# When tile 0's dot products and the second table's rows are fetched in a one-core decoder step

## The chip, the cores and the metric

One core of a Trainium2 chip runs the whole program. The metric is the device time in microseconds of one execution. Three executions of the kernel before gave a median of 2046.18 us (2037.33 to 2052.13). A fourth, profiled one took 2047.33 us; its span from first to last instruction is 2045.5 us, and all rows below are of that one.

Five engines work side by side: TensorE (PE: matrix products, with PEld for its weight loads), VectorE (DVE), ScalarE (ACT), GpSimd (POOL) and SyncE (SP). POOL and SP only start transfers here. Each engine runs its own instructions in order; semaphores order them among each other.

## What is computed

The reference is one layer of a decoder on 512 prompt tokens and 32 sample tokens (8 sequences of 4 tokens). Cut to what matters:

```python
h = rmsnorm(x, attn_norm)
u, vn, q, k, v = mix_projection(h, w_in, ln_g, ln_b, pos)       # one projection feeds both mixers
a_out = gmlp_chunk(u, vn, w_s, b_s)
b_out = combine_branches(dilated window attention of q, k, v)   # sample tokens also read the cache
x = x + concatenate([a_out, b_out]) @ w_out
x = x + peer_ffn(rmsnorm(x, ffn_norm), w_q, sub_keys, u_tab, v_tab)
y = rmsnorm(x, final_norm)

def peer_ffn(x, ...):                      # for each token, 8 heads
    s = scores of x @ w_q against 2 x 128 keys
    top 16 of the 16 x 16 sums of the two top-16 lists -> eid, 16 of 16384 experts
    g = softmax(top scores)
    hid = gelu(dot(u_tab[eid], x))         # 128 rows of 1024 numbers for each token
    return sum over experts of g * hid * v_tab[eid]
```

All is float32. Each token reads 128 rows (4 KB each) of the first table u_tab and 128 of the second table v_tab; for 544 tokens that is 570 MB of the 670 MB that the kernel moves.

## The kernel before

The tokens are five tiles: tiles 0 to 3 are 128 prompt tokens each, tile 4 the 32 samples. The program is written out by hand, engine by engine.

Order of the work. Tile 0 is projected, attends, and has its output projection, queries and key scores first, ahead of all else (to about 146 us of the span). From then on the first table's rows of tile 0 can be fetched while the rest of the mixer runs: the projection of tiles 1 to 4 (to 299 us), then `attend(NG0, NG)`, the attention of tiles 1 to 3 and the samples (302 to 492 us). After attention come the output projections of tiles 1 to 4 (`project_out(t, c)` for two column halves c), their queries and key scores (13 more jobs, `queries(i)` and `key_scores(i)`, with 13 loads of `w_q`, the first 3 of which are started before attention ends), and the rest of the experts' work.

Experts. A fetch of the first table (`gather_u`) brings one row for each of 128 tokens, 0.52 MB, into a ring of UR = 6 buffers; DVE forms the 128 dot products with one instruction (L1431 in `dots_to`) and frees the buffer (`u_free`). There are 128 such fetches per prompt tile and 32 for the samples. A fetch of the second table (`gather_v`) brings the 128 rows of one token into a ring of VR = 6; PE multiplies it with that token's weights (`weigh`, L774) and frees it (`v_free`). The weights of tile t exist only once all dots of tile t are done: then come ACT's `gelu(t)`, DVE's `weights(t)`, PE's `turn_weights(t)`, ACT's `copy_weights(t)` and PE's `start_sum(t)`. `weigh_first(n)` makes the next n of tile 0's 128 weighings, and `made[0]` counts them. The 16 first-table fetches of a head wait until DVE has routed that head: `route(k)`, k = 8 t + h, is a chain of some 20 small instructions and needs the key scores of tile t, head h.

POOL's list. All fetches are started by POOL in one fixed order: the 128 first-table fetches of tile 0, then V_LEAD second-table fetches of tile 0, then first-table fetches of tile 1 alternating with the remaining second-table fetches of tile 0, and so on, tile t + 1 of the first table with tile t of the second. A fetch waits for a free buffer of its ring, and all behind it wait too.

Dots within attention. Attention runs over 26 groups: 18 pairs of heads, and after each second pair one sample sequence (8 of them). DVE makes for each group `mask_max`, `between(i, 0)`, `normalise`, `between(i, 1)`; `experts_between` puts dots there, as many as `dots_in_group(i, j)` says, from number 68 on, and at groups 1, 4 and 10 (`ROUTE_ATT`) one `route`. The samples read their cache: `load_vc(b)` fills a single buffer and starts only when the outputs of the sequence before are done.

Other tables. `NORM_AT` gives the dot before which DVE makes `norm_x2(t)` (the norm of tile t ahead of its queries). `ROUTE_STEP` gives, for group g of 16 dots, which heads are routed in it (head 10 after dot 136, 11 at 152, 12 at 168, 13 at 184, and so on). `EID_FIRST` is the number of tile 0's weighings that are made before PE turns tile 1's expert numbers (`turn_eid(1)`).

## Time and profile before

| | |
|---|---|
| median of three runs | 2046.18 us (2037.33 to 2052.13) |
| the profiled execution | 2047.33 us, span 2045.5 us |
| PE busy | 1513.8 us (74%), granted clock 0.913 of full |
| DVE busy | 1087.3 us (53%) |
| POOL busy | 1044.0 us (51%), 1088 of its 1119 instructions are table fetches |
| ACT busy | 215.8 us (11%) |
| DMA | 670 MB, 328 GB/s over the span; q0 (POOL's) 571.78 MB, q1 (SP's) 97.16 MB |

How to read it: a timeline row has the start, the length (us), the engine, the line, the operation, what is written and read, the count, and in brackets how long the engine had been idle and what released it. A POOL row is the time it takes to start a fetch, not to bring it. "L774 x4" is one weighing (two column halves, each in two passes). A row of the windows view gives, for a stretch of the span, each engine's busy time, then the granted TensorE clock, the busy share of the DMA engines, and GB/s.

### The profile page before, as it was taken

How to read it: one execution, taken by the hardware profiler on the slowest of the kernel's cores; microseconds unless marked ns; L12 is line 12 of the kernel's file. 1: busy time of each engine (PE TensorE's matmuls, PEld its weight loads, DVE VectorE, ACT ScalarE, POOL GpSimd, SP SyncE). 2: the span in 40 equal slices, each digit the busy share in tenths (PEclk: the TensorE clock that was granted, in tenths of full speed). 3: DMA queues.
4: the chain of work that ended last, by engine and by line, in shares of the span. 5: the costliest groups of instructions: out<-in, count | busy, mean ns of one | idle time of the engine just before them, and what ended most of it. 6: DMA issues, size and time to landing. Idle time of an engine off the chain costs nothing.

```text
span 2045.5 us, 16501 instructions
## 1 busy us (share of the span) xinstructions
PE 1513.8 (74%) x5398; PEld 547.7 (27%) x5398; DVE 1087.3 (53%) x2879; ACT 215.8 (11%) x610; POOL 1044.0 (51%) x1119
## 2 busy tenths in 40 slices
PE   7889977678977777775666676665666666777997
PEld 4475644444432223431111111111111111111221
DVE  2257868783356545526655556666666666422000
ACT  2411123343100000010100000010000000100000
POOL 3032332341555546346566666665555556666664
PEclk9799997778999889898899999998999888899999
DMA  9587868998998779769799999997888889999997
GB/s 320 198 315 253 310 248 328 343 405 329 332 385 329 279 282 377 297 230 377 288 369 372 357 368 357 360 382 284 325 317 321 323 319 339 342 367 363 370 363 280
DMA packets 213254, 670.00 MB, mean 328 GB/s; under 512 B 19600, under 2 KB 54656, under 8 KB 213040
## 3 DMA queue, kind: packets, MB, share of 16 engines
q0 software_dynamic: 157728, 571.78, 74.0%
q1 hardware_dynamic: 55440, 97.16, 13.3%
q8 instruction: 43, 0.70, 0.1%
q14 instruction: 43, 0.35, 0.0%
HBM read 663.26 MB, written 5.60 MB: 327 GB/s over the span
## 4 chain that ended last, share of the span: by engine, by line
PE 28%; DVE 19%; issue 16%; DMA 15%; POOL 14%; another core or an unknown queue 5%; ACT 2%; DVEq 0%; SPq 0%; ACTq 0%; POOLq 0%
POOL area_r L1576 14%; PE bank L774 10%; PE bank L549 6%; DMA area_r<-in_v_tab,eidT 6%; DMA area_r<-in_u_tab,eid 6%; DVE area_r L1431 6%; PE bank L719 3%; PE bank L672 2%; DMA area_w<-in_v_cache 2%; DVE area_w L1360 1%; DVE area_w L1358 1%; DVE rt L1361 1%; PE bank L492 1%; DVE rtu L1331 1%
## 5 line engine op out<-in xcount | busy, mean ns | idle before, releaser
L774 PE MATMUL bank<-area_r,area_c 128*32 128x512 f32 (+1 forms) x1632 | 697.5, 630 | 253.8 <-DMA area_r<-in_v_tab,eidT 223.1
L1431 DVE CUSTOM_DVE_ANT_0 area_r<-area_r,bank 128x1024 f32<-128x1024 f32 x544 | 648.0, 1217 | 423.3 <-DMA area_r<-in_u_tab,eid 364.4
L1576 POOL DMA_INDIRECT area_r<-in_u_tab,eid x544 | 515.1, 947 | 616.1 <-DVE hid L1431 381.1
L1576 POOL DMA_INDIRECT area_r<-in_v_tab,eidT x544 | 513.4, 944 | 369.9 <-PE bank L774 153.4
L774 PE MATMUL bank<-area_r,area_v 128*32 128x512 f32 (+1 forms) x544 | 285.1, 650 | 119.1 <-DMA area_r<-in_v_tab,eidT 107.2
L774 PEld LDWEIGHTS bank<-area_r,area_c 128*32 128x32 f32 (+1 forms) x1632 | 136.8, 111 | 788.3 <-DMA area_r<-in_v_tab,eidT 464.0
L549 PE MATMUL bank<-area_w,area_t 128*128 128x384 f32 (+1 forms) x448 | 160.8, 515 | 12.7 <-issue 8.5
L719 PE MATMUL bank<-area_t,area_w 128*128 128x128 f32 (+2 forms) x672 | 134.0, 360 | 22.6 <-ACT area_x L878 19.3
L774 PEld LDWEIGHTS bank<-area_r,area_v 128*32 128x32 f32 (+1 forms) x544 | 51.1, 114 | 312.5 <-DMA area_r<-in_v_tab,eidT 197.1
L719 PEld LDWEIGHTS bank<-area_t,area_w 128*128 128x128 f32 x672 | 101.9, 203 | 54.2 <-issue 42.6
L549 PEld LDWEIGHTS bank<-area_w,area_t 128*128 128x128 f32 x448 | 85.3, 194 | 78.8 <-issue 29.7
L878 ACT ACTIVATE area_x<-bank 128x384 f32<-128x384 f32 (+8 forms) x136 | 52.5, 409 | 397.1 <-PE bank L774 141.7
L1449 DVE RECIPROCAL small<-small 128x1 f32<-128x1 f32 x5 | 0.8, 160 | 143.8 <-ACT small L1106 143.8
L1073 ACT ACTIVATE tops<-tops 128x128 f32<-128x128 f32 (+1 forms) x5 | 1.5, 307 | 612.1 <-DVE rt L1361 354.3
L672 PE MATMUL bank<-area_w,area_t 128*128 128x512 f32 x128 | 59.3, 619 | 1.4 <-ACT area_t L878 0.7
L573 PE MATMUL bank<-area_r 64*128 64x128 f32 (+3 forms) x96 | 30.7, 716 | 25.3 <-DVE att L1273 23.3
L1431 DVE DVE_READ_ACCUMULATOR2_ANT hid<- 128x1 f32 x544 | 44.3, 81 | 0.0
L1264 DVE CUSTOM_DVE_ANT_0 area_x<-bank,area_c 128x256 f32<-128x256 f32 (+4 forms) x52 | 25.9, 535 | 30.4 <-PE bank L573 25.7
L878 ACT ACTIVATE area_t<-bank 64x128 f32<-64x128 f32 (+5 forms) x121 | 32.1, 276 | 73.0 <-PE bank L492 34.0
L1078 ACT ACTIVATE hid<-hid 128x128 f32<-128x128 f32 (+1 forms) x5 | 1.5, 293 | 353.7 <-DVE hid L1431 180.1
L878 ACT ACTIVATE area_w<-bank 128x256 f32<-128x256 f32 (+2 forms) x36 | 14.3, 399 | 213.3 <-PE bank L737 93.3
L1349 DVE MAX8 rt<-area_w 128x8 f32<-128x256 f32 (+1 forms) x40 | 17.0, 426 | 35.5 <-remote 25.9
(168 smaller groups left out, 1006.2 us busy)
## 6 DMA issues: line engine op xcount, KB each, us to landing
area_w<-in_w_q SPq DMA_DIRECT2D x21, 1024.0 KB, 8.0
area_w<-in_w_in SPq DMA_DIRECT2D x12, 1536.0 KB, 10.5
area_w<-in_k_cache SPq DMA_DIRECT2D x8, 1920.0 KB, 19.2
area_w<-in_v_cache SPq DMA_DIRECT2D x8, 1920.0 KB
area_r<-in_u_tab,eid POOLq DMA_INDIRECT x544
area_r<-in_v_tab,eidT POOLq DMA_INDIRECT x544
area_w<-in_w_out SPq DMA_DIRECT2D x4, 2048.0 KB, 9.6
area_w<-in_w_in SPq DMA_DIRECT2D x2, 2048.0 KB, 14.3
```

Source lines behind the costliest of these rows:

```text
L492: return pe.transpose(out, src, ident[0:n, 0:n])
L549: mm = pe.matmul(out_half(u)[0:n, 0:w], featT[:, k, a:a + n], w_now[:, k, 0:w], start=(k == 0), stop=(k == KD - 1))
L573: mm = pe.matmul(score_psum(u, n), qT[r0:r0 + HD, pr, t * P:(t + 1) * P], kT[r0:r0 + HD, pr, 0:n], start=True, stop=True)
L672: mm = pe.matmul(ps[0:n, :], featT[:, k, a:a + n], w(k, c * 512, (c + 1) * 512), start=(k == 0), stop=(t == 0 and k == KD - 1))
L719: mm = pe.matmul(half(4 + c)[:, 0:n], w[:, k, c * P:(c + 1) * P], featT[:, k, a:a + n], start=(k == 0), stop=(k == KD - 1))
L774: mm = pe.matmul(acc[CG * g:CG * g + m, e, :], wd[g][:, c * CG:c * CG + m], v_ring[s][:, e * 512:(e + 1) * 512], start=False, stop=False, ...
L878: return nc.scalar.activation(out, src, ACT.Copy, scale=scale)
L1264: return vec.tensor_tensor_reduce(out=out, in0=scores, in1=counts, scale=-1.0, scalar=3e38, op0=ALU.add, op1=ALU.min, accum_out=least)
L1331: vec.max_index(idx[c][0:n, 0:8], val[c][0:n, 0:8], sc[c])
L1358: link(vec.tensor_tensor(hot[0:n], digits[0:n].unsqueeze(3).to_broadcast(four), iota[0:n, :].rearrange("p (a b k) -> p a b k", a=1, b=1).t ...
L1431: vec.tensor_tensor_reduce(out=u_ring[s], in0=u_ring[s], in1=x_cur, scale=1.0, scalar=0.0, op0=ALU.mult, op1=ALU.add, accum_out=hid[t % 2] ...
L1576: nc.gpsimd.indirect_dma_start(out=ring[s], out_offset=None, in_=table, in_offset=bass.IndirectOffsetOnAxis(ap=where, axis=0)).then_inc(la ...
```

## The change

Attention holds 16 of tile 0's dots (2 before each sample group) in place of 59, so the dots reach number 84 there, not 127; the route groups too have their 2. The other 44 dots follow behind attention in `block.vector`, with the routes of heads 8 and 9 put after dots 112 and 120, and the norm of tile 1 before dot 100. Tile 0's weights come only then, so PE's `turn_weights(0)` and `start_sum(0)` move behind `project_out(2, 0)`, the 36 weighings that stood ahead of `project_out(2, 0)` and the four right behind it are gone from there, and ACT's `gelu(0)` and `copy_weights(0)` move likewise. In the jobs 8 to 12 `key_scores(i - 1)` now comes behind `queries(i)`, on PE and ACT. `v_free` is given its 6 buffers right after attention. V_LEAD goes from 30 to 6. The norms of tiles 2, 3, 4 come before dots 136, 142, 148 (they were at 152, 158, 165), and EID_FIRST from 104 to 100.

```diff
--- before.py
+++ after.py
@@ -64,11 +64,11 @@
 ROUTE_STEP = ({g: [g + 2] for g in range(8, 14)} | {15: [16], 16: [17, 18]} | {g: [g + 2] for g in range(17, 24)}
               | {g: [2 * g - 22, 2 * g - 21] for g in range(24, 31)})
 TOPS_ATT = 16
-NORM_AT = {SLOTS + 24: 2, SLOTS + 30: 3, SLOTS + 37: 4}
-V_LEAD = 30
+NORM_AT = {100: 1, SLOTS + 8: 2, SLOTS + 14: 3, SLOTS + 20: 4}
+V_LEAD = 6
 EARLY = 5
 EID_AT = 92
-EID_FIRST = 104
+EID_FIRST = 100
 
 
 def build(nc, x_p, x_s, k_cache, v_cache, gains, w_in, ln_gb, w_sT, b_sT, w_out, w_q, keysT, u_tab, v_tab,
@@ -328,11 +328,8 @@
         def dots_in_group(i, j):
             if not NG0 <= i < NG:
                 return 0
-            sample = ATT[GROUP[i][0]][0] == "s"
             before = i + 1 < NG and ATT[GROUP[i + 1][0]][0] == "s"
-            if j == 0:
-                return 2 if sample else 1
-            return 5 if before and i - NG0 not in ROUTE_ATT else 0
+            return 2 if j == 1 and before else 0
 
 
         JOBS = ([(h, [0]) for h in range(HEADS)] + [(h, [1]) for h in range(EARLY)]
@@ -831,25 +828,26 @@
             turn_eid(0)
             pe.wait_ge(w_out_again[0], 16)
             project_out(1, 0)
-            turn_weights(0)
+            pe.wait_ge(w_out_again[1], 16)
+            project_out(1, 1)
             pe.wait_ge(eidT_ready, 1)
-            start_sum(0)
-            pe.wait_ge(w_out_again[1], 16)
-            project_out(1, 1, 8)
-            weigh_first(8)
             turn_xn(1)
             pe.wait_ge(xnT_ready, 4)
             pe.wait_ge(x2_ready, 4)
             for i in range(HEADS, EARLY_END):
                 queries(i)
-                weigh_first(4)
-                key_scores(i)
+                if i > HEADS:
+                    key_scores(i - 1)
+            key_scores(EARLY_END - 1)
             for c in range(2):
                 pe.wait_ge(q_copied[c], EARLY_END)
             pe.wait_ge(s_ready, scores_through(EARLY_END - 1))
             for t in range(2, NT + 1):
                 if t < NT:
-                    project_out(t, 0, 4)
+                    project_out(t, 0, 4 if t > 2 else 0)
+                    if t == 2:
+                        turn_weights(0)
+                        start_sum(0)
                     project_out(t, 1, 4)
                 if t >= 3:
                     turn_xn(t - 1)
@@ -1151,20 +1149,23 @@
             clear(2)
             clear(3)
             attend(NG0, NG)
-            gelu(0)
             act.wait_ge(pv_done, len(ATT))
             act.wait_ge(v_out, 16 * (NT + 1))
             act.wait_ge(masked, len(ATT))
             clear(0)
             clear(1)
-            copy_weights(0)
             read_out(1)
             square_x2(1)
             copy_xnT(1)
             for i in range(HEADS, EARLY_END):
                 copy_q(i)
-                copy_s(i)
+                if i > HEADS:
+                    copy_s(i - 1)
+            copy_s(EARLY_END - 1)
             for t in range(2, NT + 1):
+                if t == 2:
+                    gelu(0)
+                    copy_weights(0)
                 if t < NT:
                     read_out(t)
                     square_x2(t)
@@ -1514,16 +1515,17 @@
                 dots_to(min(made_dots[0] + dots_in_group(i, j), SLOTS))
 
             attend(NG0, NG, experts_between)
-            dots_to(SLOTS)
             dve.wait_ge(pv_done, len(ATT))
             dve.sem_inc(v_free, VR)
             copy_eidT(0)
+            dots_to(112)
+            route(HEADS)
+            dots_to(120)
+            route(HEADS + 1)
+            dots_to(SLOTS)
             weights(0)
-            norm_x2(1)
             dve.wait_ge(xn_ready, 2)
             set_x(1)
-            route(HEADS)
-            route(HEADS + 1)
             for t in range(1, NT):
                 for h in range(STEPS[t]):
                     g = FIRST[t] + h
```

Three places show the order of instructions before and after. The first is PE's order from the end of attention: L492 (L489 of the change) is a turn (eidx: expert numbers, hid: weights, area_v: the normed tile), L672 (L669) with L681 (L678) an output projection's half, L759 (L756) `start_sum`, L774 (L771) weighings, L719 (L716) `queries`. Before:

```order
L492 MATMUL bank<-ident,eidx 128x128
L672 MATMUL bank<-area_w,area_t 128x512 x8
L681 MATMUL bank<-area_x,ident 128x512
L492 MATMUL bank<-ident,hid 128x128
L759 MATMUL bank<-area_w,ident 128x512 x2
L672 MATMUL bank<-area_w,area_t 128x512 x8
L681 MATMUL bank<-area_x,ident 128x512
L774 MATMUL bank<-area_r,area_c 32x512 x6
L774 MATMUL bank<-area_r,area_v 32x512 x2
L774 MATMUL bank<-area_r,area_c 32x512 x6
```

In the change, with rows left out where `queries`, `key_scores` and `project_out` follow each other:

```order
L489 MATMUL bank<-ident,eidx 128x128
L669 MATMUL bank<-area_w,area_t 128x512 x8
L678 MATMUL bank<-area_x,ident 128x512
L489 MATMUL bank<-ident,area_v 128x128 x8
L716 MATMUL bank<-area_t,area_w 128x128 x32
...
L489 MATMUL bank<-ident,hid 128x128
L756 MATMUL bank<-area_w,ident 128x512 x2
L669 MATMUL bank<-area_w,area_t 128x512 x8
L678 MATMUL bank<-area_x,ident 128x512
L771 MATMUL bank<-area_r,area_c 32x512 x6
L771 MATMUL bank<-area_r,area_v 32x512 x2
```

Weighings began right behind the projection of tile 1. They now begin behind that of tile 2, after all of the jobs 8 to 12.

The second is POOL's list from the first table's rows of tile 0 on. Before:

```order
L1576 DMA area_r<-in_u_tab,eid 128x1024 x128
L1576 DMA area_r<-in_v_tab,eidT 128x1024 x30
L1576 DMA area_r<-in_u_tab,eid 128x1024 x2
L1576 DMA area_r<-in_v_tab,eidT 128x1024
L1576 DMA area_r<-in_u_tab,eid 128x1024
L1576 DMA area_r<-in_v_tab,eidT 128x1024
L1576 DMA area_r<-in_u_tab,eid 128x1024
L1576 DMA area_r<-in_v_tab,eidT 128x1024
L1576 DMA area_r<-in_u_tab,eid 128x1024 x2
```

In the change:

```order
L1578 DMA area_r<-in_u_tab,eid 128x1024 x128
L1578 DMA area_r<-in_v_tab,eidT 128x1024 x6
L1578 DMA area_r<-in_u_tab,eid 128x1024 x2
L1578 DMA area_r<-in_v_tab,eidT 128x1024
L1578 DMA area_r<-in_u_tab,eid 128x1024
L1578 DMA area_r<-in_v_tab,eidT 128x1024
L1578 DMA area_r<-in_u_tab,eid 128x1024
L1578 DMA area_r<-in_v_tab,eidT 128x1024
L1578 DMA area_r<-in_u_tab,eid 128x1024
```

The lead of the second table fell from 30 to 6, and the two tables now alternate one to one in place of 1.3 to one.

The third is DVE's order around the mask of a sample group (L1264 with 96x640; L1265 of the change) in attention; L1431 (L1432) is a dot, two rows each. Before, behind four more such pairs of rows:

```order
L1431 ISA area_r,hid<-area_r,bank 128x1024
L1431 ISA hid 128x1
L1264 ISA area_x,att<-bank,area_c 96x640
L1264 ISA att 96x1
L1264 ISA area_x,att<-bank,area_c 96x32
L1264 ISA att 96x1
L1273 TENSOR_TENSOR att<-att 96x1
L1431 ISA area_r,hid<-area_r,bank 128x1024
L1431 ISA hid 128x1
L1431 ISA area_r,hid<-area_r,bank 128x1024
L1431 ISA hid 128x1
L1279 RECIPROCAL att<-att 96x1
```

In the change, at the same group:

```order
L1432 ISA area_r,hid<-area_r,bank 128x1024
L1432 ISA hid 128x1
L1432 ISA area_r,hid<-area_r,bank 128x1024
L1432 ISA hid 128x1
L1265 ISA area_x,att<-bank,area_c 96x640
L1265 ISA att 96x1
L1265 ISA area_x,att<-bank,area_c 96x32
L1265 ISA att 96x1
L1274 TENSOR_TENSOR att<-att 96x1
L1280 RECIPROCAL att<-att 96x1
```

Five dots ahead of the mask became two, and the two behind it are gone.

## Rows read from the trace of the kernel before

**Rows 1.** Windows view: busy us by engine, then clock, DMA share, GB/s.
```profile
core 0: us, PE busy (x) PEld busy (x) DVE busy (x) ACT busy (x) POOL busy (x), PEclk, DMA share, GB/s
302.00:491.60 189.60, 133.90 (x1085) 79.05 (x1083) 139.55 (x417) 79.99 (x267) 52.22 (x54) 0.76 0.96 362
491.60:609.40 117.80, 104.91 (x426) 46.95 (x425) 47.69 (x141) 13.87 (x32) 62.63 (x66) 0.98 0.91 338
609.40:680.70 71.30, 52.20 (x249) 18.68 (x248) 37.91 (x83) 10.67 (x24) 37.38 (x40) 0.86 0.83 314
680.70:961.70 281.00, 203.84 (x637) 85.57 (x637) 150.45 (x357) 18.90 (x47) 147.21 (x157) 0.90 0.81 307
961.70:1341.50 379.80, 250.91 (x520) 47.66 (x519) 229.01 (x571) 7.17 (x13) 243.42 (x258) 0.94 0.94 356
430.00:460.00 30.00, 22.19 (x168) 13.80 (x170) 24.62 (x66) 12.06 (x42) 12.46 (x13) 0.73 1.03 404
```

**Rows 2.** Timeline of PE: the turns of the weights of tiles 0, 1, 2.
```profile
500.14 0.27 PE L492 MATMUL bank<-ident,hid 128*128 128x128 f32 x1
...
961.73 0.33 PE L492 MATMUL bank<-ident,hid 128*128 128x128 f32 x1
...
1341.49 0.33 PE L492 MATMUL bank<-ident,hid 128*128 128x128 f32 x1
```

**Rows 3.** Timeline of POOL: two fetches of the second table in a row.
```profile
496.16 0.94 POOL L1576 DMA_INDIRECT area_r<-in_v_tab,eidT  x1 [0.30 <-issue]
497.41 0.94 POOL L1576 DMA_INDIRECT area_r<-in_v_tab,eidT  x1 [0.30 <-issue]
```

**Rows 4.** Waits view, 680 to 962 us, of DVE and of POOL.
```profile
DVE rt L1328 <- ACT area_w L878: 15.4, 1, 15.4
...
POOL area_r L1576 <- PE bank L774: 49.8, 5, 31.2
```

**Rows 5.** Timeline of PE: whole query jobs with no weighing between.
```profile
851.34 9.69 PE L719 MATMUL bank<-area_t,area_w 128*128 128x288 f32 x32 [2.47 <-ACT area_x L878]
...
863.41 8.00 PE L719 MATMUL bank<-area_t,area_w 128*128 128x288 f32 x32 [0.84 <-ACT area_x L878]
```

**Rows 6.** Waits view, 302 to 492 us, of PE: totals, times, longest.
```profile
PE bank L573 <- DVE att L1273: 23.3, 5, 7.7
PE bank L633 <- DMA area_w<-in_v_cache: 8.6, 3, 4.8
```

**Rows 7.** Timeline of DVE: dots ahead of a sample group's mask, in attention.
```profile
421.16 1.22 DVE L1431 CUSTOM_DVE_ANT_0 area_r<-area_r,bank 128x1024 f32<-128x1024 f32 x1
422.30 1.22 DVE L1431 CUSTOM_DVE_ANT_0 area_r<-area_r,bank 128x1024 f32<-128x1024 f32 x1
...
425.73 0.82 DVE L1264 CUSTOM_DVE_ANT_0 area_x<-bank,area_c 96x640 f32<-96x640 f32 x1
```

**Rows 8.** Timeline of PE in attention: a pair's scores, two samples' outputs.
```profile
426.91 1.22 PE L573 MATMUL bank<-area_r 64*128 64x256 f32 x4 [4.14 <-DVE att L1273]
...
436.48 2.35 PE L633 MATMUL bank<-area_w,area_x 128*32 128x256 f32 x30 [0.93 <-DMA area_w<-in_v_cache]
...
459.10 4.00 PE L633 MATMUL bank<-area_w,area_x 128*32 128x256 f32 x30 [2.78 <-DMA area_w<-in_v_cache]
```

**Rows 9.** The page's part 6: direct loads, count, KB each, us to landing.
```profile
area_w<-in_w_q SPq DMA_DIRECT2D x21, 1024.0 KB, 8.0
...
area_w<-in_k_cache SPq DMA_DIRECT2D x8, 1920.0 KB, 19.2
```

**Rows 10.** Timeline of DVE: first instruction of a route, first behind it.
```profile
311.36 0.48 DVE L1328 MAX8 rt<-area_w 128x8 f32<-128x128 f32 x2
...
321.13 0.82 DVE L1264 CUSTOM_DVE_ANT_0 area_x<-bank,area_c 96x640 f32<-96x640 f32 x1
```

**Rows 11.** Timeline of PE: a half output projection, a half query job.
```profile
586.80 7.10 PE L672 MATMUL bank<-area_w,area_t 128*128 128x512 f32 x16 [0.68 <-issue]
...
680.72 5.85 PE L719 MATMUL bank<-area_t,area_w 128*128 128x416 f32 x16 [0.37 <-ACT area_t L878]
```

## The prediction, made before the kernel ran

> **What bounds the kernel now.** I read the windows view by stage first. Attention (302.0 to 491.6 us) takes 189.6 us, from there to the turn of tile 1's weights at 961.7 us it is 470.1 us, and the next stage, tile 2 of the first table beside tile 1 of the second, takes 379.8 us [rows 1, 2]. No engine is full in any of them: PE is busy 66 to 89%, DVE 40 to 74%. What is nearly full is the pair of POOL and the DMA engines. Two fetches in a row start 1.245 us apart [rows 3]; one of 0.524 MB takes 1.30 us at the 404 GB/s of the fullest stretch [rows 1]. So a pair of fetches costs 2.5 to 2.6 us at best, and 128 pairs 320 to 333 us. Stage two of the experts needs 379.8, or 2.97 a pair. The stage that the change rebuilds is worse: from 680.7 to 961.7 us POOL starts 147.21 / 0.94 = 157 fetches [rows 1, 3], 1.79 us each. The waits view says why: DVE waits 15.4 us for a copy of key scores, with POOL's list shut behind it, and POOL waits 31.2 us for a weighing [rows 4] while PE makes three whole query jobs with none between [rows 5].
>
> Attention has another limit. At 404 GB/s it is short of DMA in part of the time [rows 1], and then the sample's value cache comes late: PE waits 8.6 us for it. It waits 23.3 us more for scores that DVE has not masked yet [rows 6], since dots stand ahead of the mask [rows 7].
>
> The sum is made against the profiled execution (2047.3 us), which is 1.1 us above the median.
>
> **Attention.** The 90 fetches that can be started in it (84 dots and 6 buffers) are 38 fewer than 128, 49 us of DMA at 1.30. That is not what attention saves: it saves only PE's waits.
> - In the four sample groups that have no route near them, five dots ahead of the mask become two. Dots start 1.14 us apart [rows 7], so the mask comes 3.4 us earlier; PE's wait of 4.14 us in such a place goes to under 1 [rows 8]. With some 1.8 us at a second such place that is 5 us.
> - The cache: per sample 3.9 MB of keys and values are loaded [rows 9]. With nine dots beside them that is 8.6 MB, 21 us, which is the present distance between samples (436.5 to 459.1 us [rows 8] is 22.6). With two dots it is 5.0 MB, 12 us. The 8.6 us of waits go.
> - After such waits the clock is low: the same 30 matmuls took 4.00 us behind a wait of 2.78 us and 2.35 behind 0.93 [rows 8]. Two of these give 3 us, other slow stretches some 3 more.
> - At groups 1, 4 and 10 the route of 9.8 us [rows 10] stands ahead of the mask. There two dots are taken away, of which one stood ahead of the mask, and two are added behind the route, so the mask comes 1.1 us later. I put three such groups at -1 us of saving each, partly made up by the dots gone elsewhere: together -1.
> Sum: 5 + 8.6 + 6 - 1 = 19, taken as 20 us with the small waits. Bounds: 5 (only half of the cache waits go, the rest is latency between engines) and 49 (all of the DMA time moved out). I stay near the waits, since DVE and PE chains remain. Attention ends at about T = 471.6.
>
> A rule of the Trainium skill bears on the size of a fetch. The rows show 404 GB/s over 30 us with tables, caches and weights mixed [rows 1]. The page "DMA: Bandwidth & Descriptors", section "Where 436 GB/s comes from", says that for HBM to SBUF a core's share of HBM, about 358 GB/s, binds. The trace disagrees in this stretch. By that figure a fetch would be an estimated 1.46 us, and the 38 moved ones 6 us dearer than I take them.
>
> **From T to the weights of tile 0.** DVE makes 44 dots at 1.14 (50 us), two routes (19.5), the norm and `eidT` (3). From dot 90 to 112 it follows the fetches at 1.30 in place of 1.14 (+4), since the ring held only six. That is 77, with two waits of 1 us 79. PE is hidden: two half projections of 8 us, then turns, then five jobs of about 5.5 us end near T + 52, in time for the route at T + 39; it then makes `project_out(2, 0)` and stands idle for some 20 us. Before, DVE was busy only 47.7 of 117.8 us in this place [rows 1], so these dots fill idle time of DVE. But DMA has nothing to do from about T + 83 to T + 94: six rows of the second table and two of the first are in, and the seventh waits for the first weighing.
>
> **From there to the first large query job.** PE turns the weights and starts the sum (4 us), makes the second half of tile 2 (7.1 + 1 [rows 11], 9 with a slow start), and then does what took 71.3 us from 609.4 to 680.7 [rows 1], with four weighings behind each half. The norm of tile 2 now stands behind the route after dot 136 (up to 10 us), and the norm of tile 4 waits for first-table fetch 147, which needs 18 of the 20 weighings. Against this, the rows that PE waited for in that stretch come at one to one, not at 1.3 to one. I add 2: 86 us, to T + 165. Ends: 74 (the waits for rows vanish) and 100 (both norms are paid whole).
>
> **From there to tile 1's weights.** 108 weighings are left, 6 with rows landed: 104 pairs. At the 2.97 us of the next stage [rows 1] they take 309. Six loads of `w_q` of 1.05 MB [rows 9] add 16 (2.6 each at 404 GB/s). The next stage holds 8 routes in 128 pairs, this one 5 in 104, 1.5 fewer in proportion; its 61 us above POOL's pace are 7.6 a route, so 11 go. DVE no longer waits for scores: job 13's stand after 36 weighings, when fetch 165 is out, and are wanted at dot 184. All eight jobs carry eight weighings, so the gap of 31.2 us is gone. That is 314; I take 312. Ends: POOL's pace, 208 x 1.245 + 16 = 275, and the present 1.79 us a fetch, 372.
>
> Sum: 79 + 86 + 312 = 477 against 470.1, 7 us longer with 38 more fetches in it. What follows is the same program with the same one-to-one list and takes the 1083.8 us that it took. Total: 2047.3 - 20 + 7 = 2034, against the median 2033.
>
> **The rivals.**
> 1. *POOL's pace is reached.* The coupled waits were all that held the last part back, so 104 pairs run at 2.7 us (281 + 16 = 297), and attention gains 30: 2047 - 30 + 79 + 86 + 297 - 470 = 2009, and below if more. For it: 888 to 961 us ran near the full DMA rate before. Against: the next stage, free of these waits, does not reach it. 0.25.
> 2. *The late start costs more than attention gives.* All 128 weighings now stand behind T + 79, and each route shuts a one-to-one list for both rings. It decides where the last part runs at over 3.2 us a pair: at 3.3 it is 343 + 16 = 359 without a credit for routes, and with 10 us of attention gained: 2047 - 10 + 79 + 86 + 359 - 470 = 2091; at 3.1 it is 2070. For it: the hole of DMA at T + 83 and the two norms. Against: 15.4 and 31.2 us of waits that go [rows 4]. 0.2, mostly near 2072.
> 3. *The change does nothing to attention.* Its pace is set by the routes and PE's slow clock (0.76 [rows 1]), 5 us gained, the rest as forecast: 2049. 0.15.
> The forecast itself: 0.4, from 2018 to 2052.
>
> **How the numbers follow.** A difference of 1% (20.5 us) is about what a measurement of this kernel can tell from none. Faster than 2025.7: rival 1 and a fifth of the forecast, 0.33. Slower than 2066.6: rival 2 and a little, 0.22. Between: 0.45. The range takes in rival 1's 2009 and most of rival 2: 2005 to 2072.
>
> **What would show it.** Attention (first pair's scores to the turn of `eidx`) near 170 us, no wait of PE for the value cache, POOL idle longer in it. DVE making dots without a break for 25 to 30 us behind it; the turn of tile 0's weights 79 us after attention's end, then 10 to 14 us with no fetch started. The three last query jobs with weighings between, no wait of DVE for scores over 5 us, and the turn of tile 1's weights at about 949 us. The stage behind it at 380. The forecast is wrong if attention stays above 180, if the last part is over 335 or under 290 us, or if the stages from tile 1's weights on change by more than 10 us.

## The result and the profile after

The kernel after the change took 2073.04 us (median of 4 runs, 2072.4 to 2074.33), the kernel before, beside it, 2049.16 us. The ratio is 1.0127, with a 95% interval of 1.0084 to 1.0171: **slower by 1.3%**. I had forecast 2033, 0.65% faster, and the time lies just outside my range. A later group of runs, on another chip, gave 1.0015 (1.0001 to 1.0030); two traces of one program that differ so are what much of the account below rests on.

The windows view of the kernel after, by stage (attention; to the turn of tile 0's weights; to the first large query job; the eight jobs; to the turn of tile 1's weights; the stage behind it). Columns as in [rows 1]:

```profile
304.99:464.88 159.89, 119.09 (x1085) 70.92 (x1085) 91.89 (x329) 79.94 (x268) 14.98 (x16) 0.83 0.81 300
464.88:547.26 82.38, 52.19 (x244) 37.04 (x244) 69.92 (x161) 12.61 (x27) 40.82 (x43) 0.84 0.96 350
547.26:628.32 81.06, 53.54 (x271) 24.27 (x272) 38.51 (x83) 13.01 (x30) 41.77 (x44) 0.82 0.81 299
628.32:871.20 242.88, 164.46 (x624) 83.54 (x628) 115.45 (x282) 15.11 (x42) 123.31 (x131) 0.86 0.82 309
871.20:993.11 121.91, 82.14 (x178) 15.33 (x170) 65.35 (x143) 3.56 (x5) 76.68 (x82) 0.93 0.90 338
993.11:1372.89 379.78, 261.71 (x519) 48.91 (x519) 229.15 (x571) 7.17 (x13) 241.03 (x257) 0.93 0.93 355
```

| stretch | before | forecast | after |
|---|---|---|---|
| attention | 189.6 | 169.6 | 159.9 |
| attention's end (T) to tile 0's weights | 8.5 | 79 | 82.4 |
| from there to the first large job | 180.6 | 86 | 81.1 |
| from there to tile 1's weights | 281.0 | 312 | 364.8 |
| next stage | 379.8 | 379.8 | 379.8 |

One row is far off: the last part, 53 us over the forecast. It falls into eight query jobs (242.9 us, 30 each, with 64 weighings in them) and 44 bare weighings (121.9, 2.77 a pair). The bare weighings are as fast as forecast; the jobs are not, and their DMA share is only 0.82. The timeline shows PE and ACT in the key scores of one of these jobs:

```profile
674.45 1.16 PE L734 MATMUL bank<-area_r,area_x 128*128 128x128 f32 x8
679.54 0.38 ACT L876 ACTIVATE area_w<-bank 128x256 f32<-128x256 f32 x1 [34.90 <-remote]
679.98 0.71 PE L734 MATMUL bank<-area_r,area_x 128*128 128x128 f32 x4 [4.37 <-issue]
685.20 0.38 ACT L876 ACTIVATE area_w<-bank 128x256 f32<-128x256 f32 x1 [5.28 <-remote]
685.64 1.06 PE L734 MATMUL bank<-area_r,area_x 128*32 128x128 f32 x4 [4.95 <-issue]
686.64 0.64 ACT L876 ACTIVATE area_w<-bank 128x256 f32<-128x256 f32 x2 [1.05 <-remote]
```

Two tiles' scores are computed by 675.6 us (the profile models the end of a product), but ACT, which has nothing else to do, copies the first at 679.54 and the next only at 685.20; PE needs each copy before it can use that half of PSUM again. What takes 2.9 us at its quickest takes 12. The copy waits for no work: the view has it released by "remote", which stands where the releasing event comes too late behind any instruction for the profile to put it down to one. I call this a **late handoff**. In the 242.9 us PE stands so for over 2.5 us at nine places, 59.8 us together. In the meantime no weighing is made, the six buffers of the second table fill, and POOL's list shuts. The next weighing starts at 695.11 us, the next fetch at 697.29:

```profile
687.82 7.36 PE L716 MATMUL bank<-area_t,area_w 128*128 128x416 f32 x16 [1.12 <-ACT area_x L876]
697.29 0.94 POOL L1578 DMA_INDIRECT area_r<-in_v_tab,eidT  x1 [13.96 <-PE bank L771]
```

The windows of that place show DMA going from full to nothing:

```profile
682.00:686.00 4.00, 0.36 (x2) 0.33 (x3) 1.73 (x4) 0.38 (x1) 1.03 (x2) 0.50 1.03 408
686.00:690.00 4.00, 2.88 (x7) 1.37 (x6) 1.59 (x3) 1.44 (x4) 0.00 (x0) 0.50 1.03 410
690.00:694.00 4.00, 4.00 (x12) 2.18 (x11) 2.10 (x4) 0.00 (x0) 0.00 (x0) 0.88 0.24 92
694.00:698.00 4.00, 4.00 (x23) 1.51 (x22) 0.00 (x0) 0.00 (x0) 0.71 (x1) 1.00 0.00 0
```

The waits view of 628 to 871 us gives the sums:

```profile
ACT area_w L876 <- remote: 80.1, 12, 34.9
POOL area_r L1578 <- PE bank L771: 68.9, 9, 14.0
...
PE bank L716 <- ACT area_x L876: 25.7, 5, 9.9
...
PE bank L771 <- DMA area_r<-in_v_tab,eidT: 12.2, 8, 2.3
```

(ACT's 34.9 holds its ordinary idle time before a job's scores too; 5 us are the late part.) POOL's 68.9 us of waits for a weighing stand where [rows 4] has 49.8, of which one was 31.2. The last row matters too: PE waits only 12.2 us for rows of the second table. Its 242.9 us are 164.5 of work, some 63 of waits for handoffs and 12 for rows, so it is PE's own chain of work and waits that sets the length of the jobs. I did not make that sum when I wrote the theories.

### The profile page after: what moved, and what is told of

The parts are those of the page before. It is cut to its first block, busy times and chain, and to the rows that moved or that the text cites. A ratio compares the mean times of both kernels' runs of the same rounds, so it can differ in the third digit from the quotient of the medians.

```text
span 2070.6 us, 16504 instructions
## 1 busy us (share of the span) xinstructions
PE 1500.8 (72%) x5398; PEld 549.0 (27%) x5398; DVE 1093.2 (53%) x2879; ACT 216.2 (10%) x611; POOL 1038.8 (50%) x1119
## 4 chain that ended last, share of the span: by engine, by line
PE 24%; DVE 20%; issue 16%; DMA 15%; POOL 14%; another core or an unknown queue 8%; ACT 2%; DVEq 0%; SPq 0%; ACTq 0%; POOLq 0%
POOL area_r L1578 14%; PE bank L771 8%; DMA area_r<-in_u_tab,eid 8%; PE bank L546 6%; DVE area_r L1432 6%; DMA area_r<-in_v_tab,eidT 5%; PE bank L716 3%; DMA area_w<-in_v_cache 2%; PE bank L669 1%; PE bank L489 1%; DVE area_w L1359 1%; DVE area_w L1361 1%; DVE rt L1362 1%; PE bank L630 1%
## 5 line engine op out<-in xcount | busy, mean ns | idle before, releaser
L1432 DVE CUSTOM_DVE_ANT_0 area_r<-area_r,bank 128x1024 f32<-128x1024 f32 x544 | 648.0, 1217 | 477.7 <-DMA area_r<-in_u_tab,eid 423.6
L771 PE MATMUL bank<-area_r,area_c 128*32 128x512 f32 (+1 forms) x1632 | 695.4, 630 | 233.3 <-DMA area_r<-in_v_tab,eidT 208.0
L771 PE MATMUL bank<-area_r,area_v 128*32 128x512 f32 (+1 forms) x544 | 281.2, 643 | 115.9 <-DMA area_r<-in_v_tab,eidT 103.9
L771 PEld LDWEIGHTS bank<-area_r,area_c 128*32 128x32 f32 (+1 forms) x1632 | 137.0, 112 | 767.3 <-DMA area_r<-in_v_tab,eidT 457.3
L716 PE MATMUL bank<-area_t,area_w 128*128 128x128 f32 (+2 forms) x672 | 147.3, 383 | 48.8 <-ACT area_x L876 32.1
L716 PEld LDWEIGHTS bank<-area_t,area_w 128*128 128x128 f32 x672 | 110.3, 219 | 87.3 <-issue 65.8
L771 PEld LDWEIGHTS bank<-area_r,area_v 128*32 128x32 f32 (+1 forms) x544 | 50.3, 112 | 302.2 <-DMA area_r<-in_v_tab,eidT 193.4
L546 PEld LDWEIGHTS bank<-area_w,area_t 128*128 128x128 f32 x448 | 85.1, 194 | 82.6 <-issue 32.7
L669 PE MATMUL bank<-area_w,area_t 128*128 128x512 f32 x128 | 58.2, 610 | 1.4 <-ACT area_t L876 0.7
L734 PE MATMUL bank<-area_r,area_x 128*128 128x128 f32 (+1 forms) x160 | 27.6, 310 | 31.4 <-issue 17.0
L1265 DVE CUSTOM_DVE_ANT_0 area_x<-bank,area_c 128x256 f32<-128x256 f32 (+4 forms) x52 | 26.1, 538 | 43.0 <-PE bank L570 33.0
L570 PE MATMUL bank<-area_r 64*128 64x128 f32 (+3 forms) x96 | 26.6, 628 | 24.8 <-DVE att L1274 22.8
L1432 DVE DVE_READ_ACCUMULATOR2_ANT hid<- 128x1 f32 x544 | 44.3, 81 | 0.0
```

The lines of the kernel that those rows point to most:

```text
L546: mm = pe.matmul(out_half(u)[0:n, 0:w], featT[:, k, a:a + n], w_now[:, k, 0:w], start=(k == 0), stop=(k == KD - 1))
L570: mm = pe.matmul(score_psum(u, n), qT[r0:r0 + HD, pr, t * P:(t + 1) * P], kT[r0:r0 + HD, pr, 0:n], start=True, stop=True)
L669: mm = pe.matmul(ps[0:n, :], featT[:, k, a:a + n], w(k, c * 512, (c + 1) * 512), start=(k == 0), stop=(t == 0 and k == KD - 1))
L716: mm = pe.matmul(half(4 + c)[:, 0:n], w[:, k, c * P:(c + 1) * P], featT[:, k, a:a + n], start=(k == 0), stop=(k == KD - 1))
L734: mm = pe.matmul(ps, col, keys[:, (2 * h + c) * NKEYS:(2 * h + c + 1) * NKEYS], start=True, stop=True)
L771: mm = pe.matmul(acc[CG * g:CG * g + m, e, :], wd[g][:, c * CG:c * CG + m], v_ring[s][:, e * 512:(e + 1) * 512], start=False, stop=False, ...
```

## The experiments

Ratios are against the kernel before in the same group. Neither of the two kernels was traced in groups 1 and 2, so stage times there are held against the traces of the first measurement.

**Theory A:** PE is away from the second table for some 19 us per job (12 us of key scores with late handoffs, 6 to 7 of the next half queries), and six buffers cover six pairs, 15 us; the rest is lost. **Theory B:** the one-to-one list or the routes pace the part. **Theory C:** the late handoffs cost by themselves, wherever the weighings stand.

### Group 1: spreading, attention alone, fewer bytes

All beside the kernel before at 2034.34 us.

```diff
 def key_scores(i, between=0):        # in the loop over its tiles, behind mm.then_inc(s_done, 1)
+    weigh_first(between * (ts.index(t) + 1) // len(ts) - between * ts.index(t) // len(ts))
...                                  # in the loop over the late jobs
+more = i + 1 < len(JOBS) and made[0] + 8 <= EID_FIRST
-    queries(i + 1, 4 if made[0] + 8 <= EID_FIRST else 0)
-key_scores(i)
+    queries(i + 1, 2 if more else 0)
+key_scores(i, 4 if more else 0)
```

> The changed kernel, with the eight weighings of a late query job laid two behind each half of the queries and four between the tiles' key scores, in place of four behind each half. If PE's absence from the second table (some 19 us of key scores and half queries, longer than the six buffers cover) made the jobs 30.3 us each (theory A): jobs 24 to 25 us each, the part from the first large job to the turn of tile 1's weights 310 to 325 us in place of 364.8, the whole 2025 to 2040 us. If the one-to-one list (second table only six rows ahead) or the routes pace the part (theory B): 360 to 370 us and 2070 us, since neither list nor routes are touched. If handoffs are late by themselves and each late one holds up everything behind it (theory C): no gain either, the jobs stay at 28 to 30 us.

Measured: ratio 0.9938 (0.9906 to 0.9971). In the windows view the eight jobs and the weighings behind them are

```profile
624.31:821.40 197.09, 171.75 (x622) 80.38 (x624) 107.64 (x263) 15.06 (x41) 118.54 (x127) 0.94 0.94 357
821.40:949.67 128.27, 85.32 (x177) 15.97 (x174) 72.77 (x163) 3.94 (x6) 81.91 (x88) 0.96 0.93 355
```

Jobs 24.6 us each, the part 325.4. These are theory A's numbers; B falls, since list and routes are untouched. Late handoffs are not gone (PE waits 7.32 us before 702.18, 4.17 before 796.55), and C falls in its strong form. But the two are not parted cleanly. PE's waits of over 2.5 us went from 59.8 us to 14.6, which is all that the jobs gained. Counted at ACT, whose start doesn't depend on what PE does meanwhile, there were 11 starts over 1.5 us late in the jobs of the changed kernel (49.8 us) and 4 here (18.6 us). So a part of the gain is late handoffs that did not occur, and only the rest is weighings laid over them. Why fewer occur is not shown.

> The kernel before with the same spreading in its query jobs that carry weighings (the last three carry none and stay as they are). Theory A: its jobs with weighings get shorter by some 3 us each, 10 to 20 us in all: 2030 to 2040 us. Theories B and C: 2046 to 2050 us, no difference.

Measured: 0.9898 (0.9828 to 0.9969), its jobs 185 us against 205. The upper end of A's 10 to 20 us.

The third run takes only the new `dots_in_group` into the kernel before.

> The kernel before with only the new sharing of dots in attention (16 in it, 44 made in one block behind it, before tile 0's weights); projections, turns, jobs and the list of fetches as before. Attention: 160 to 163 us in place of 189.6. Turn of tile 0's weights some 60 us after attention's end in place of 8.6, since nothing but DVE's 44 dots and two POOL-paced ones stand there, with PE idle for about 45 us. If attention's gain is whole and the late start costs what stands bare: -28 + 50, the whole 2065 to 2075 us. If the 44 dots fill time that was idle anyway: 2020 to 2035 us.

Measured: 1.0159 (1.0081 to 1.0238), with attention at 159.2 us, 61.3 from there to tile 0's weights (8.5 before), and the two stretches behind at 176.6 and 282.0. So attention's 30 us are real, and 52 us of bare dots behind it cost more. In the change, projections and early jobs run beside that block. From T to the first large job it takes 163.5 us, against 189.1 before and 237.9 here, but with 20 weighings in it in place of 60, so how much is hidden and how much only moved behind can't be read from this.

The fourth cuts `for i in range(HEADS + 3, len(JOBS))` in SP's loads of `w_q` to `HEADS + 6`, and PE no longer waits for the loads that are gone.

> The changed kernel without the six loads of query weights for the late jobs (their queries use the weights that lie in the buffers, so later experts are chosen otherwise). If DMA's bytes pace the part from the first large job to tile 1's weights: 16 us shorter (6 x 2.6), 348 us, the whole 2057 us. If the loads, started right ahead of the key scores, are what makes the handoffs late and opens the holes: 40 us or more shorter, 2030 us. If PE's absence alone counts (theory A): 0 to 10 us shorter, 2063 to 2073 us, with the holes behind the key scores still there.

Measured: 1.0044 (1.0009 to 1.0079), 17 us under the changed kernel; the part is 350.1. That is the price of the bytes, as I had put it (16). PE's waits of over 2.5 us for a handoff in the jobs still sum to 47 us: the loads are not the cause.

### Group 2: bytes, buffers, and the other half

Beside the kernel before at 2034.76 us.

```diff
-gather(v_ring, i % VR, v_tab, eidT[:, a:a + 1], v_landed)
+(for 12 <= i < 128)  out=v_ring[i % VR][:, 0:512], in_=v_tab.rearrange("e (two d) -> (e two) d", two=2)
```

> The changed kernel, where the fetches of the second table for tile 0 from the 13th on bring rows of 2 KB in place of 4 KB (another view of the table, so half of each row is wrong or old), with the same number of fetches, weighings and waits. The DMA time of a pair falls from 2.6 to some 2.0 us. If the late handoffs between PE and ACT in the key scores (4 to 10 us) come from full DMA engines: they fall towards 1 us, and the eight jobs go from 30.3 to 20 to 24 us each. If they come from something else in the program: the handoffs stay at 4 to 10 us and the jobs at 28 us or more, though DMA has half the bytes.

Measured: 1.0012 (0.9981 to 1.0043). The jobs take 229 us, and PE waits over 2.5 us for a handoff at eight places, 54.5 us together, nearly as in the kernel after. DMA is still full around those places (share 1.02, 390 GB/s at 700 to 704 us), as pairs are only fetched earlier. So 30 MB less buy 1.15% or 23 us (1.0012 for 1.0127) and leave the handoffs nearly as they are. The first alternative is wrong in its numbers, but the cause isn't separated by this.

With `VR = 5` and `V_LEAD = 5`:

> The changed kernel with five buffers in place of six for the second table. If PE's absence beyond what the buffers cover sets a job's time (theory A), each job grows by one pair's time, 2.5 us: the eight jobs 255 to 268 us in place of 242.7, and more in the stages behind, where each stop of PE counts too. If handoffs alone (theory C) or DVE's first-table side sets it, the jobs stay within 5 us of 242.7.

Measured: 1.0297 (1.0229 to 1.0365), jobs 255.7 us (+12.8), and PE's waits for rows of the second table in them 29.5 us in place of 12.2. With the spread weighings:

> The same five buffers with the spread weighings. Theory A: PE is never away longer than a half of the queries (5.9 us and a score piece), which five buffers cover as well as six: the jobs within 5 us of the 196.8 us of the spread kernel. If buffers are short in general: 10 to 20 us longer.

Measured: 1.0033 (0.9987 to 1.0080), jobs 202 us (+5), the whole part 326.1 against 325.4. In the jobs a buffer less costs where PE is long away and little where it isn't. Both fit A, the first at the low edge of its range. But the whole is 0.95% longer than the spread version's, and that loss lies elsewhere: from tile 2's weights to the end both versions with five buffers take 715 to 716 us, where a version with six took 696 on the same chip (attention_back, the run below). I had not forecast its size, and no run says which stop makes it.

> The changed kernel with the old sharing of dots in attention (59 in it), everything behind it as changed. Attention 187 to 190 us. The block behind it falls by up to 44 dots (50 us) but not below PE's own work of some 52 us: turn of tile 0's weights 55 to 60 us after attention's end in place of 82.4. Whole: +29 - 25, 2065 to 2080 us; if the fetches saved from the block come back as DMA time in attention alone, the jobs behind stay at 30 us each and 364.8 us.

The edit also puts the norm of tile 1 ahead of dot 112. Measured: 1.0136 (1.0093 to 1.0179), attention 190.7, then 59.5 to tile 0's weights, 78.3, 360.3. The same time as the changed kernel: in this order, moving 44 dots out of attention brings 30 us and costs 23 us in the block, 3 behind it and 4.5 in the last part. So the loss against the kernel before lies in the rest of the change. That it is the weighings that moved behind, and not the list or the order of the jobs 8 to 12, is my reading; no run takes these one by one.

### Group 3: a pause before the scores, and better versions

Here the kernel before took 1884.35 us, 7% less than on the chips of the groups ahead: another chip. Ratios within the group stand.

```diff
-    queries(i + 1, 4 if made[0] + 8 <= EID_FIRST else 0)
-key_scores(i)
+    queries(i + 1)
+key_scores(i)
+weigh_first(8 if made[0] + 8 <= EID_FIRST else 0)
```

> The changed kernel with all eight weighings of a late job behind its key scores, none inside the queries. PE then computes two halves of the next queries (8.3 to 11.7 us) before the key scores, so the fetches that the last weighings set free have mostly landed when the scores start. PE's absence from the second table is at least 11 to 14 us even with quick handoffs. If the late handoffs (4 to 10 us) come only while fetches keep the DMA engines full: key scores take 2 to 3 us again, as in the kernel before at 738.84 us, PE is away 11 to 15 us, about what six buffers cover, and the eight jobs take 200 to 215 us in place of 242.7; the whole 2030 to 2045 us. If the handoffs are late in this program whatever DMA does: PE is away for 20 us or more and the jobs stay at 240 us or grow; the whole 2070 us or more.

Measured: 1.0065 (1.0041 to 1.0088), key scores of 2.4 us without one late handoff, jobs 191.7 us. It looked like the first alternative, but nothing on this chip said that the order had done it.

> The kernel before, with the 40 weighings that are left behind the first late query job spread over all seven jobs (five or six each, most of them between the key scores) in place of eight each in five jobs and none in the last two or three. Theory A: PE is never away from the second table for long and the idle DMA time of the last jobs goes too: 2000 to 2012 us, 5 to 10 us under the spread version of the kernel before. If the last jobs' bare key scores were no loss, since their time is made up by full buffers: the same as that one, 0.990 of before.

Measured: 0.9825 (0.9806 to 0.9845), 32.5 us faster. I had expected 2000 to 2012 us against some 2034, so this is the upper end in microseconds, though on a chip without late handoffs. Its jobs take 160.5 us with DMA full to the end.

```profile
652.35:812.80 160.45, 154.56 (x540) 72.87 (x540) 101.79 (x238) 15.46 (x42) 98.99 (x106) 1.00 1.00 382
```

The next one has 4 in place of 2 in `dots_in_group`, and the spread weighings.

> The changed kernel with spread weighings and 32 dots in attention in place of 16. Each dot moved back costs attention 0.68 us (29.7 us for 44) and takes 1.14 us or more off the block behind it, while PE's own work of 52 us doesn't bound: attention +11, block -18 to -20, so 7 to 9 us less than the spread kernel, ratio 0.990. If dots in attention cost most where the first four are added at each sample: attention +20 and no gain, 0.994.

Measured: 1.0115 (1.0091 to 1.0140), wrong in both terms. Attention took 182.0 us with 16 more dots, 1.5 us each and not 0.68, with PE waiting 31.5 us for DVE. The block stayed at 80.6 us: dots now reach number 100 in attention, and there stands the norm of tile 1, for which DVE waits 20.7 us (to 490.92 us, with T at 469.4).

### Groups 4 and 5: the changed kernel on a quick chip

Both groups fell on one chip, where the kernel before took 1884.53 and 1885.51 us.

> The changed kernel, on the chip of this group of runs, so that the versions can be held against it directly. Ratio to before 1.013 (the interval measured was 1.008 to 1.017); jobs 243 us, late handoffs (a wait of PE for ACT of 3 to 10 us in the key scores) at seven to nine places.

Measured: **1.0015 (1.0001 to 1.0030)**, against what I expected. The program that lost 1.3% loses next to nothing. The timeline of one job:

```profile
754.69 1.81 PE L734 MATMUL bank<-area_r,area_x 128*128 128x128 f32 x12
757.34 4.12 PE L716 MATMUL bank<-area_t,area_w 128*128 128x288 f32 x16 [0.85 <-ACT area_x L876]
761.39 1.93 PE L771 MATMUL bank<-area_r,area_c 128*32 128x512 f32 x12
```

and of ACT in it:

```profile
755.44 0.83 ACT L876 ACTIVATE area_w<-bank 128x256 f32<-128x256 f32 x2 [23.87 <-PE bank L734]
756.53 0.37 ACT L876 ACTIVATE area_w<-bank 32x256 f32<-32x256 f32 x1 [0.27 <-PE bank L734]
```

The stages of the kernel after, and then of the kernel before (from attention; T to the first large job; jobs; weighings), both on that chip:

```profile
287.13:447.62 160.49, 118.52 (x1085) 70.99 (x1085) 91.90 (x329) 80.00 (x268) 14.98 (x16) 0.83 0.82 303
447.62:530.25 82.63, 53.13 (x244) 37.35 (x245) 69.99 (x161) 12.62 (x27) 40.90 (x44) 0.83 0.97 351
530.25:611.71 81.46, 55.57 (x272) 24.48 (x272) 38.51 (x83) 13.03 (x30) 41.15 (x44) 0.81 0.77 297
611.71:801.10 189.39, 166.97 (x622) 76.50 (x624) 107.97 (x263) 15.47 (x42) 119.10 (x127) 0.99 0.97 374
801.10:914.08 112.98, 81.29 (x178) 15.42 (x174) 71.59 (x163) 3.56 (x5) 80.50 (x87) 1.00 1.02 399
914.08:1253.11 339.03, 245.90 (x519) 46.76 (x519) 229.17 (x571) 7.17 (x13) 243.40 (x257) 0.99 1.01 399
```

```profile
286.39:471.91 185.52, 134.82 (x1084) 79.77 (x1085) 139.18 (x417) 80.02 (x268) 52.28 (x54) 0.75 0.98 374
471.91:648.04 176.13, 153.89 (x674) 65.95 (x675) 91.36 (x248) 24.79 (x56) 103.44 (x108) 0.98 0.93 353
648.04:828.30 180.26, 148.26 (x528) 72.99 (x532) 101.27 (x238) 15.47 (x42) 93.53 (x99) 0.96 0.86 329
828.30:905.27 76.97, 49.68 (x114) 9.09 (x109) 44.34 (x96) 3.56 (x5) 52.50 (x56) 0.94 0.93 357
905.27:1245.47 340.20, 246.96 (x520) 46.89 (x519) 228.32 (x569) 7.17 (x13) 242.54 (x256) 0.98 1.01 396
```

The jobs of the kernel after are 189.4 us here and 242.9 on the first chip, 53.5 apart, and the bare weighings 9 us. PE works as long in these jobs on both (167.0 and 164.5 us); what is gone are its waits of over 2.5 us (59.8 us there, none here). At 167.0 of 189.4 us PE is close to full even so. Neither kernel has a single "remote" wait in the waits view here, and in the jobs no wait of PE for ACT is over 1.1 us. On the first chip the kernel after has such rows for ACT, POOL and DVE:

```profile
ACT area_w L876 <- remote: 86.2, 13, 34.9
ACT area_x L876 <- remote: 43.8, 5, 14.5
POOL area_r L1578 <- remote: 33.8, 15, 4.7
DVE rt L1350 <- remote: 31.1, 12, 4.0
```

What hardly depends on such handoffs takes the same time on both chips: the block of dots (82.4 and 82.6 us), the start of a fetch (every 1.24 us).

> Weighings two and two in the queries and four between the key scores. Ratio to before 0.994 as on the first chip. Theory A says that it and the version with all eight behind the scores come out within 0.5% of each other, since in both PE is away no longer than the six buffers cover; if many short absences are better than one of 14 us, this one is 10 us or more faster.

Measured: 1.0022 (1.0007 to 1.0037). No gain over the changed kernel, and 0.33% from the version with all eight behind (1.0055, next), within theory A's 0.5%: where key scores, handoffs and half a query together keep PE away for only 7 to 9 us (1.81 + 0.85 + 4.12 in the rows above), six buffers cover it, and there is nothing to win. Theory A needs the late handoffs, and they need that kind of chip.

> All eight weighings of a late job behind its key scores, beside the changed kernel on one chip. If the quick handoffs that its first run showed come from the order of the program and not from that faster chip: no wait of PE for ACT over 3 us in the key scores, the jobs 195 to 205 us, ratio to before 0.995 to 1.005, so 0.8% to 1.8% below the changed kernel. If that chip alone made them quick: waits of 4 to 10 us here too, jobs of 230 us or more and a ratio of 1.013.

Measured: 1.0055 (1.0028 to 1.0082), and in a third measurement 1.0068 (1.0050 to 1.0086), with jobs of 197.4 and 199.4 us. Not under the changed kernel but 0.4 to 0.5% over it; on this chip every version has quick handoffs, so what quickens them on the other kind stays untried.

> The changed kernel with all eight weighings of a late job behind its key scores. On a chip of 2034 to 2049 us: if handoffs are late only while fetches are in flight, the key scores are quick here too, and the jobs take 200 to 215 us in place of 242.7 (ratio 0.995 to 1.005); if they are late whatever DMA does, 240 us or more (1.013 or more). On a chip of 1885 us: 1.0055 as before.

The same change of order in the kernel before, with its last 40 weighings shared out:

```diff
-    queries(i + 1, 4 if made[0] + 8 <= EID_FIRST else 0)
-key_scores(i)
+    queries(i + 1)
+key_scores(i)
+if i + 1 < len(JOBS):
+    weigh_first(-(-(EID_FIRST - made[0]) // (len(JOBS) - 1 - i)))
```

> The kernel before with its 40 last weighings laid five or six behind the key scores of each of the seven last jobs, none in the queries. Theory A: as fast as with the weighings spread between the scores of all seven jobs, ratio 0.980 to 0.990. If one absence of 11 to 14 us per job is too long for its list (1.3 first-table rows to one of the second): 0.990 to 1.000.

> The kernel before with its last 40 weighings laid five or six behind the key scores of each of the last seven jobs. On a chip of 2034 to 2049 us: at or under the spread version's 0.990, so 0.975 to 0.990. On a chip of 1885 us: 0.980 as before.

Measured: 0.9799 (0.9782 to 0.9815) and 0.9814 (0.9797 to 0.9830), 1848.73 and 1851.92 us. **This version beats the kernel before** by 34 to 36 us, and so the changed one (1.0015). Both measurements are of this chip; on one with late handoffs it was not run. Its jobs and what follows:

```profile
651.61:803.10 151.49, 134.48 (x540) 71.42 (x540) 97.73 (x232) 15.45 (x42) 94.07 (x100) 0.98 1.00 385
803.10:877.76 74.66, 48.39 (x97) 8.91 (x98) 47.98 (x102) 3.56 (x5) 51.60 (x56) 0.96 0.99 387
```

Against 180.3 and 77.0: jobs that all carry weighings keep DMA full, where the kernel before had a share of 0.86.

> The kernel before once more, for its trace on the chip of this group, ratio 1. If this is a chip on which it takes some 1885 us: all key scores of its late jobs quick (2.5 us and no wait of PE for ACT over 1 us), the part from the first late job to the turn of tile 1's weights 262 to 270 us in place of 281, and the part from attention's end to there 430 to 440. If it is one on which it takes 2034 to 2049 us: waits of 3 to 9 us at three places and 281 us, as in the first trace.

Measured: 1.0005 (0.9994 to 1.0015), with the rows above; the jobs and the weighings together 257.2 us, a little under the expected range, and 433.4 from attention's end.

## Why the prediction was wrong

- **Attention.** Forecast -20, measured -29.7 (-25.0 on the quick chip). The direction was right, the terms only in part. PE's waits for scores fell from 23.3 us to 22.8 where I had put 5 (29.1 to 22.8 on the quick chip), and 22 of what is left stand at the three route groups. Its waits for the cache fell from 8.6 to 4.2 and did not go (5.3 and 5.3 on the quick chip). Too small was the term of the clock: the same 1085 products kept PE busy for 133.9 us at a granted clock of 0.76 before and for 119.1 at 0.83 after (134.8 and 118.5 on the quick chip), 15 to 16 us where I had 6. And 10 us that I had not counted are PE's waits for ACT. The waits view of PE in attention, of the kernel before and then of the kernel after, has them and the scores:

```profile
PE bank L619 <- ACT area_t L878: 16.8, 9, 5.2
...
PE bank L570 <- DVE att L1274: 22.8, 4, 9.3
PE bank L616 <- ACT area_t L876: 6.6, 9, 1.7
```

  On the quick chip both kernels have 6.6 us there, so that term seems to be late handoffs.
- **T to tile 0's weights.** Forecast 79, measured 82.4 and 82.6. Right, with PE's wait for it (11.34 us) and the pause of DMA behind it.
- **To the first large job.** Forecast 86, measured 81.1. PE waits 12 us for the norm of tile 2 and 13 for the last turn, as feared.
- **To tile 1's weights.** Forecast 312, measured 364.8. This is the step that failed. I priced the 108 weighings by a stage in which PE does nothing but weigh, 2.97 a pair, and took it that eight query jobs fit in beside at no cost but the bytes of `w_q`. I had rows that spoke against it: [rows 5] gives such a job's queries as 9.69 us of matmuls, and I never added up PE's own time, nor asked what a handoff costs with fetches in flight. In the eight jobs PE works 164.5 us and stands 59.8 us at nine places in waits of 3 to 10 us, which makes them 242.9 us. Without such waits they take 189.4 on the quick chip, so these waits are the size of the error. That the part took 302.4 there, near 312, is luck: with that chip's pace of 2.65 a pair my own working gives some 281.
- **What follows.** Forecast unchanged, measured 379.8 for 379.8, and the rest 698 for 704. Right, and inside my bound of 10 us.
- **The rivals.** Rival 2 gave the sign: over 3.2 us a pair, and it was 3.35 ((364.8 - 16) / 104). Its reason was another. It put the cost on the late start and the routes, and the spread version, with both, needs 325 us and is 0.6% faster than the kernel before: 0.9938 of my base of 2046 is 2033. That this is the time that I had forecast is chance, since it is another program. Rival 1's pace of 2.7 was nearly reached on the quick chip ((302.4 - 16) / 104 = 2.75), but there the kernel before is quicker too.
- **What I held it against.** I compared the new part with a measured 470.1 us, as if that had no such losses. On the quick chip the same stretch of the kernel before takes 433.4, 37 us less than on the first chip; the changed kernel loses 62 between the two (528.2 against 466.5). The change did not bring late handoffs in; it has 64 weighings in jobs with them, where some 40 stood. Without them the balance is -25.0 in attention and +33.1 behind it, where I had -20 and +7: even there nothing is left of the gain that I forecast, and the balance from T on is a second error, which late handoffs don't explain.

## What to carry over

A stage in which one engine serves a ring and makes short round trips with another is to be priced twice: by the engine's own sum of work and waits, and by how long it stays away from the ring at one stretch, against the ring's depth times the pace. Lay the ring's work between the round trips, or share it out over all of them, so that none is left bare (before_behind, 2% on the quick chip). And a difference of 1% may belong to a chip: compare on a second one before a story is made of it.

## What the runs showed of the hardware

- In the first measurement and in groups 1 and 2 an engine now and then started late behind the instruction that it waited for; on the two chips of groups 3 to 5 this was not seen in ten traces. By the start and end times in the trace of the kernel after on the first chip, starts over 1.5 us late are ACT behind PE (19, 88 us together), POOL behind PE (12, 24 us) and DVE behind its own instructions (36, 83 us). On the quick chip the same program has none, one and none. PE behind ACT shows in attention of the kernel before (16.8 us of waits against 6.6). Since DVE waits so for itself, it is not only the modelled ends of PE's products. Of the 67, 65 fell where the DMA share was over 0.9; in windows of 4 us it is that high in 71% of the span. Where DMA ran dry it did not happen on the first chip either: at 738.84 us of the kernel before, where POOL had started nothing for a while, four tiles' scores were made and copied in 2.9 us. Its windows there:

```profile
738.00:740.00 2.00, 2.00 (x10) 1.01 (x8) 0.00 (x0) 0.36 (x1) 0.00 (x0) 0.76 0.79 260
740.00:742.00 2.00, 1.31 (x9) 0.88 (x8) 1.62 (x10) 1.41 (x5) 0.00 (x0) 1.00 0.01 2
```

  So it seems to need full DMA engines, but they are as full on the quick chip, and no run isolated that. Without the loads of `w_q`, or with half the bytes of the second table, PE's waits for handoffs in the jobs fell only from 59.8 us to 47 and 54.5. Late loading of instructions is an obvious rival: the DMA records of the kernel after have eight such loads in the eight jobs, each of 0.3 to 1.1 us, and none falls into one of the nine waits. How long a load had been asked for they don't tell. What the event is stays open. Nor is it shown that it belongs to the chip: the measurements with it came first and those without it last, so it may be something that ended in between, such as a neighbour's traffic. The traces with it also hold fewer records of semaphore updates (2560 against 3329 for the changed kernel), so the label "remote" alone proves little; the idle times and the run times are what counts.
- Engines and DMA are equally fast on both kinds: a fetch starts every 1.24 us, and full stretches move 399 to 410 GB/s. In the kernel before DVE is busy 1087.3 and 1087.8 us, and PE 1513.8 and 1478.2 at granted clocks of 0.913 and 0.945; so most of the 165 us between the spans (2045.5 and 1880.3) is waiting. The Trainium skill, page "DMA: Bandwidth & Descriptors", section "Where 436 GB/s comes from", has about 358 GB/s of HBM per core as the binding limit between HBM and SBUF. The rows of both kinds lie above it, with one core at work: 404 GB/s over 30 us on the first chip, 399 over 339 us on the quick one.
